# RWKV stage: ScalarE copies the turned groups out of alternating banks, the first inversion level goes by token half, and products outside the chain stand in the states' waits

## The reference

```
def step(state, inp):
    r_t, w_t, k_t, v_t, kk_t, b_t = inp
    sa = jnp.einsum('bhvk,bhk->bhv', state, -kk_t)
    state = (state * w_t[:, :, None, :] + sa[..., None] * b_t[:, :, None, :]
             + v_t[..., None] * k_t[:, :, None, :])
    y = jnp.einsum('bhvk,bhk->bhv', state, r_t)
    return state, y
...
y = rwkv7_scan(r_h, heads(decay), k_h, v_h, kk, a_h)
...
y = y + jnp.sum(r_h * k_h * r_k, axis=-1, keepdims=True) * v_h
...
y = y.reshape(B, S, RWKV_DIM).astype(p.dtype) * g
return y @ w_o_rwkv
```

## Time and profile before

| | |
|---|---|
| median of 3 runs | 1594.96 us (1594.63 to 1595.7) |
| profiled execution | 1595.48 us, its span 1594.2 us |
| TensorE matmul busy | 1536.3 us, 96% of the span |
| VectorE, ScalarE, GpSimd busy | 995.7, 643.6, 426.8 us |
| chain that ended last | PE 88%, DVE 4%, DMA 3%, ACT 2%, issue 2% |

### The profile page before, as it was taken

How to read it: one execution, slowest core, us unless ns; L and a number is a source line. 1 busy time by engine, 2 the same in 40 slices (tenths; PEclk the granted TensorE clock), 3 DMA queues, 4 the chain that set the end, 5 groups by cost and what they waited for, 6 DMA issues and landing times.

```text
span 1594.2 us, 25461 instructions
## 1 busy us (share of the span) xinstructions
PE 1536.3 (96%) x10035; PEld 1279.7 (80%) x10035; DVE 995.7 (62%) x1820; ACT 643.6 (40%) x994; POOL 426.8 (27%) x285
## 2 busy tenths in 40 slices
PE   8999999989999877899999999999999999999998
PEld 5777878765455577469999999999999888888887
DVE  5788787744465663439898843333333777777776
ACT  4455453532221411123444344334433554554543
POOL 0000000000000200004888888888885000000000
PEclk9999999999999987999999999999999999999999
DMA  9776664347465910334766656666664677777776
GB/s 338 254 260 215 230 230 134 132 158 258 140 206 184 396 73 12 109 138 146 187 145 147 143 139 144 146 145 140 141 146 110 200 243 236 243 236 244 235 244 228
DMA packets 166011, 297.25 MB, mean 186 GB/s; under 512 B 49475, under 2 KB 70259, under 8 KB 165893
## 3 DMA queue, kind: packets, MB, share of 16 engines
q1 hardware_dynamic: 119616, 277.08, 51.5%
q0 software_dynamic: 39296, 8.55, 7.3%
q10 hardware_dynamic: 6980, 9.99, 1.9%
HBM read 276.54 MB, written 19.03 MB: 185 GB/s over the span
## 4 chain that ended last, share of the span: by engine, by line
PE 88%; DVE 4%; DMA 3%; ACT 2%; issue 2%; SPq 0%; ACTq 0%; DVEq 0%
PE bank L515 21%; PE bank L517 20%; PE bank L519 20%; PE bank L510 9%; PE bank L1058 7%; PE bank L851 1%; PE bank L1005 1%; DMA ada_late<-in_w_ada_dram 1%; PE bank L488 1%; PE bank L567 1%; DMA slot<-in_w_in_dram 1%; PE bank L864 1%; DMA slot<-in_w_out_dram 1%; DVE gt L1165 1%; PE bank L863 0%
## 5 line engine op out<-in xcount | busy, mean ns | idle before, releaser
L2430 POOL DMA_INDIRECT c_dram<-gates,places x256 | 404.3, 1579 | 173.9 <-DVE gates L1831 96.3
L1184 DVE TENSOR_TENSOR dT_low<-bank,dT_high 128x512 fp32r<-128x512 f32 x256 | 165.1, 687 | 216.4 <-ACT dT_high L2327 215.0
L515 PE MATMUL bank<-hT_high,dT_high 128*128 128x256 f32 x1024 | 299.0, 292 | 0.1
L517 PE MATMUL bank<-hT_low,dT_high 128*128 128x256 f32 x1024 | 288.2, 281 | 0.0
L519 PE MATMUL bank<-hT_high,dT_low 128*128 128x256 f32 x1024 | 284.7, 278 | 0.0
L515 PE MATMUL bank<-up_high,A_high 128*128 128x512 f32 x512 | 200.0, 391 | 1.1 <-DVE A_low L1184 1.1
L517 PE MATMUL bank<-up_low,A_high 128*128 128x512 f32 x512 | 200.7, 392 | 0.0
L2339 ACT CAST up_high<-slot 128x1024 fp32r<-128x1024 f32 x128 | 134.3, 1049 | 164.2 <-DMA slot<-in_expert_up_dram 164.2
L519 PE MATMUL bank<-up_high,A_low 128*128 128x512 f32 x512 | 199.2, 389 | 0.0
L519 PEld LDWEIGHTS bank<-hT_high,dT_low 128*128 128x128 f32 x1024 | 193.4, 189 | 0.0
L515 PEld LDWEIGHTS bank<-hT_high,dT_high 128*128 128x128 f32 x1024 | 192.8, 188 | 0.3 <-issue 0.3
(11 more groups left out here) (431 smaller groups left out, 2294.6 us busy)
## 6 DMA issues: line engine op xcount, KB each, us to landing
slot<-in_expert_down_dram SPq DMA_DIRECT2D x128, 512.0 KB
slot<-in_expert_up_dram SPq DMA_DIRECT2D x128, 512.0 KB, 3.6
slot<-in_w_in_dram SPq DMA_DIRECT2D x41, 1024.0 KB, 5.2
P<-in_w_ada_dram SPq DMA_DIRECT2D x16, 1024.0 KB, 7.7
c_dram<-zeros SPq DMA_DIRECT2D x1, 16384.0 KB, 50.9
slot<-c_dram SPq DMA_DIRECT2D x128, 128.0 KB, 3.5
slot<-in_w_in_dram SPq DMA_DIRECT2D x6, 2048.0 KB, 8.2
ada_late<-in_w_ada_dram POOLq DMA_DIRECT2D x8, 1024.0 KB, 5.8
```

The source lines that it names most:

```text
L515: pe.matmul(o, lhsT=lhs_high.bitcast(F32R), rhs=rhs_high.bitcast(F32R), start=start, stop=False, skip_group_check=True)
L517: pe.matmul(o, lhsT=lhs_high.bitcast(F32R), rhs=rhs.bitcast(F32R), start=False, stop=False, skip_group_check=True)
L1184: return v.tensor_tensor(dst.bitcast(F32R), src, high, ALU.subtract)
L2430: g.indirect_dma_start(C_dram, bass.IndirectOffsetOnAxis(ap=places[:, x, k:k + 1], axis=0), gates[:, x, k:k + 1], None, compute_op=ALU.add ...
```

## The change

Four edits, and the bank numbers that they need:

1. The groups of `alphaT` and `kappaT` stay in banks 4 and 5, those of `rhoT` and `betaT` go to 6 and 7. ScalarE copies both groups of the first three; `betaT` is shared as before. The product `y = r * kx` on VectorE moves up, ahead of `alpha`.
2. Level 0 of the inversion is issued as n(0), x and y(0), n(1), kb(0), x and y(1), kb(1), instead of kb(0), n(0), n(1), kb(1), x and y(0), x and y(1). VectorE masks `D1` of a half at the end of that half, and `v_kb(0)` stands between its additions for half 0 and for half 1. Banks of x and y become 2t and 2t + 1. Levels 1 to 4 keep their order.
3. In each chunk all eight products of kappa with v are issued before the wait for U, and those of beta with U behind it.
4. `yd` of half 0 (`pe_inner(0)`) is issued behind s of chunk 1, `ys` of half 0 (`pe_outer(0)`) behind s of chunk 2; those of half 1 stay at the end. VectorE's additions stay where they were.

```
-    def pe_turn_bank(tag, tiles, k, size=4):
-        b = fill((tag, k), 4 + k % 4)
+    def pe_turn_bank(tag, tiles, k, size=4, first=0):
+        b = fill((tag, k), 4 + (first + k) % 4)
...
-            pe_turn(tag, tiles_of(x))
+            for k in range(2):
+                pe_turn_bank(tag, tiles_of(x), k, first=2 * (n % 2))
...
-        pe_pairs("kb", kappaT, 0, (6, 7))
...
+    def pe_level_xy(i, t):
+        bx, by = fill(("x", i, t), 2 * t) if i < 4 else None, fill(("y", i, t), 2 * t + 1)
...
+        pe_level_n(0, 0)
+        pe_level_xy(0, 0)
+        pe_level_n(0, 1)
+        pe_pairs("kb", kappaT, 0, (6, 7))
+        pe_level_xy(0, 1)
+        pe_pairs("kb", kappaT, 1, (6, 7))
+        for i in range(1, 5):
+            for t in range(TT):
+                pe_level_n(i, t)
+            for t in range(TT):
+                pe_level_xy(i, t)
...
+            for h in range(RH):
+                pe.matmul(o[h], lhsT=kappa[rows, t, at[h]], rhs=v_[rows, t, at[h]], start=(h < 2), stop=False,
+                          skip_group_check=True)
             for q in range(2):
                 clear(pe, ("ws", c, q))
             for h in range(RH):
...
+                m = pe.matmul(o[h], lhsT=beta[rows, t, at[h]], rhs=U[rows, t, at[h]], start=False, stop=(h > 5),
+                              skip_group_check=True)
             m.then_inc(filled(("s", c)), 1)
+            if c == 1:
+                pe_inner(0)
+            if c == 2:
+                pe_outer(0)
         for q in range(2):
             clear(pe, ("ws", 3, q))
+        pe_inner(1)
+        pe_outer(1)
...
+        v.wait_ge(shifted, 8)
+        v.tensor_tensor(y, r_, kx, ALU.mult).then_inc(bonus_raw, 1)
...
-        for tag, dst in (("alphaT", arT[:, :, 0, :]), ("rhoT", arT[:, :, 1, :]), ("kappaT", kappaT), ("betaT", betaT)):
-            v_turn(tag, by_tile(dst, 4), 2)
-            if tag == "rhoT":
-                v.tensor_tensor(y, r_, kx, ALU.mult).then_inc(bonus_raw, 1)
+        v_turn("betaT", by_tile(betaT, 4), 2)
...
-            if i == 0:
-                v_kb(0)
...
+                if (i, t) == (0, 0):
+                    v_kb(0)
...
+    def a_turn_one(tag, dst, k, size=4):
+        b = held(a, (tag, k))
+        a.copy(dst(k * size, size), b[:, 0:size * P].rearrange("p (k n) -> p k n", k=size)).then_inc(emptied((tag, k)), 1)
...
-            a_turn(tag, by_tile(dst, 4), 2)
+        for tag, dst in (("alphaT", arT[:, :, 0, :]), ("rhoT", arT[:, :, 1, :]), ("kappaT", kappaT)):
+            for k in range(2):
+                a_turn_one(tag, by_tile(dst, 4), k)
+        a_turn("betaT", by_tile(betaT, 4), 2)
```

More of the change, by code:

```diff
@@ L839, in pe_pairs @@
             m.then_inc(filled((tag, t, q)), 1)
-    def pe_invert():
-        for i in range(5):
-            for t in range(TT):
[L844 to L853, removed]
-            if i == 0:
-                pe_pairs("kb", kappaT, 1, (6, 7))
-            for t in range(TT):
[L857 to L867, removed]
@@ new lines, in pe_level_n @@
+    def pe_level_n(i, t):
+        b = fill(("n", i, t), 4 + t)
+        pe.wait_ge(level_masked, 2 * i + t + 1)
+        if i:
+            clear(pe, ("x", i - 1, t))
+            clear(pe, ("y", i - 1, t))
+        for h in range(RH):
+            for rows in HALF:
+                m = pe.matmul(b[rows, h * RN:(h + 1) * RN], lhsT=NMv[rows, t, h, :],
+                              rhs=XI[rows, t, h, :], start=True, stop=True)
+        m.then_inc(filled(("n", i, t)), 1)
+    def pe_level_xy(i, t):
+        bx, by = fill(("x", i, t), 2 * t) if i < 4 else None, fill(("y", i, t), 2 * t + 1)
+        clear(pe, ("n", i, t))
+        for h in range(RH):
+            for rows in HALF:
+                at = slice(h * RN, (h + 1) * RN)
+                if i < 4:
+                    mx = pe.matmul(bx[rows, at], lhsT=YI[rows, t, h, :], rhs=T1_[rows, t, h, :], start=True, stop=True)
+                my = pe.matmul(by[rows, at], lhsT=T1_[rows, t, h, :], rhs=YI[rows, t, h, :], start=True, stop=True)
+        if i < 4:
+            mx.then_inc(filled(("x", i, t)), 1)
+        my.then_inc(filled(("y", i, t)), 1)
@@ L908, in pe_states @@
             b = side(("s", c))
+            o = [b[HALF[h % 2], h // 2 * RN:(h // 2 + 1) * RN] for h in range(RH)]
+            at = [slice(h * RN, (h + 1) * RN) for h in range(RH)]
+            for h in range(RH):
+                pe.matmul(o[h], lhsT=kappa[rows, t, at[h]], rhs=v_[rows, t, at[h]], start=(h < 2), stop=False,
+                          skip_group_check=True)
             for q in range(2):
@@ new lines, in pe_states, with pe_inner, pe_outer @@
+        pe_outer(1)
+    def pe_inner(t):
+        b = side(("yd", t))
+        for h in range(RH):
+            for rows in HALF:
+                at = slice(h * RN, (h + 1) * RN)
+                pe.matmul(b[rows, at], lhsT=D1[rows, t, h, :], rhs=U[rows, t, at], start=True, stop=False)
+                m = pe.matmul(b[rows, at], lhsT=D2[rows, t, h, :], rhs=v_[rows, t, at], start=False, stop=True)
+        m.then_inc(filled(("yd", t)), 1)
+    def pe_outer(t):
+        for q in range(2):
+            b = side(("ys", t, q))
+            for h in odds[q]:
+                for cp in range(2):
+                    m = pe.matmul(b[HALF[cp], h // 2 * RN:(h // 2 + 1) * RN],
+                                  lhsT=arT[HALF[q], h // 2, 1, chunk(t, cp)],
+                                  rhs=states[HALF[q], 2 * t + cp, h // 2, :], start=True, stop=True)
+            m.then_inc(filled(("ys", t, q)), 1)
```

## The result

| | kernel before | changed kernel |
|---|---|---|
| first comparison, 5 runs each | 1595.7 us median (1594.63 to 1598.35) | 1585.51 us median (1579.53 to 1588.82) |
| ratio, 95% interval | | 0.9936 (0.9916 to 0.9956) |
| later, same kernel again, 5 runs | 1594.44 us (17 runs, 1591.06 to 1599.88) | 1584.41 us (1583.21 to 1587.0), ratio 0.9943 (0.993 to 0.9956) |

The change makes the kernel about 10 us faster. That is the direction and the order of size forecast (16.4 us, 1578.5), but the median lies outside the range given (1574.5 to 1584), and both kernels spread more than the three runs of before had shown.

The account below looks back on a forecast made before the run. TensorE, busy in 96% of the span, was taken as the bound, losing time in chain waits and at low clock. Savings 4.9 + 4.0 + 1.5 + 6.0 = 16.4 us gave a 1578.5 us median, range 1574.5 to 1584.

Parts of the forecast that it names:

- Turned groups: Turning ahead of the first pairs: only beta is still waited for, pairs start at 549.4 instead of 554.33, saving 4.9 us.
- First level: From the first pairs to n of level 1: 15.95 us instead of 19.99, saving 4.0 us.
- 9.5 + 0.1 + 0.95 + 1.55 + 1.87 + 1.99 = 15.95: Level 0: us to half 1's mask, start, n, kb(0), x and y of half 1, then the wait to next n.
- Levels 1 to 4: Later inversion levels: kb(1) fills the gap ahead of level 1, so its n starts at high clock, saving 1.5 us.
- Walk: Chunk loop from the states to o_mla: filled holes and a mostly high clock save 6.0 us.
- the forecast's 6.9: Chunk loop if the clock stays high: 3.2 us from moved products plus 3.7 from the clock.
- So a gain ahead of them is passed on whole: After the chunk loop: o_mla and y both start from the states' end, so all 16.4 us saved earlier remain.
- a transfer or a wait with a fixed date: After the states: something fixed in time could take back the whole gain, giving 1594 to 1596; none seen, chance 0.03.
- The bounds: Whole kernel: parts' limits 4.5 to 4.9, 0.5 to 4.0, 0 to 4.5, 1 to 6.9; range 1574.5 to 1584.
- rule on transposes: Turning ahead of the pairs: transposes do not bring full clock, so that part would give 4.5 us; judged contradicted by the trace.

Follow-up runs that it names:

- zero_early: Changed kernel with the 16 MB filling of the coefficient table with zeros issued one weight chunk earlier: 1582.85 us, ratio 0.9923.
- zero_late: Changed kernel with the zeros issued later, by ScalarE behind its copy of betaT, to run under the levels: 1591.79 us, ratio 0.9981.
- turn: Kernel before with only the alternating banks for turned groups, ScalarE's copies and the earlier product with kx: 1590.9 us, ratio 0.9982.
- walk: Kernel before with only kappa products ahead of the wait for U, and yd and ys of half 0 inside the chunk loop: 1587.79 us, ratio 0.9961.
- before_warm_m2: Kernel before with four extra unused matmuls in TensorE's wait for merged2: 1593.43 us, ratio 0.9993.
- warm_m2: Changed kernel with four extra unused matmuls in TensorE's 2.2 us wait for merged2: 1581.31 us, ratio 0.9907.
- old_level: Changed kernel with level 0 in its old order and the zeros issued one weight chunk earlier: 1585.95 us, ratio 0.9947.

## Why the prediction was wrong

- **Turned groups: right.** 5.2 to 5.8 us against 4.9 (3.6 to 5.0 against the other profiles of the old order); beta alone is waited for, the groups ran high (1.04 each), the product with kx and the sigmoids stayed hidden.
- **First level: the step that failed first.** The sum "9.5 + 0.1 + 0.95 + 1.55 + 1.87 + 1.99 = 15.95" had TensorE's pieces follow one another without a gap. I had no term for the zeros' traffic, since TensorE needed none of it. After the change the stage stops for 1.88 us between kb(0) and x and y of half 1, and `zero_early` and `zero_late` show that it is the zeros. In the profiles with the old order TensorE never stops there. In the kernel before the clock was low from 561.00 to 567.00, while the zeros ended at about 565, but in `turn` it was high from 555.87 on, with the zeros running to 560.5, and there was no stop either; there TensorE had waited 2.90 us ahead of kb(0). What spares the old order stays open. Of the other 1.1 us in the changed kernel 0.9 lie ahead of n of half 1: it started 10.5 us after the pairs instead of 9.6, with a low stretch of the clock (553.50 to 556.50) at the start of it. With the stop away the piece took 16.55, 16.66 and 16.72.
- **Levels 1 to 4: the number fits, the reason is not shown.** 1.5 us was forecast and 1.49 measured, twice, and n of level 1 starts high behind kb(1). But without kb(1) in the wait it ran high too, in `turn`, `walk` and `before_warm_m2` (2.08 us for its 64 matmuls, behind idle times of 1.99, 1.91 and 1.91 us); in the first profile of the kernel before it took 3.59 behind the same 1.91. Levels 1 to 4 took 29.93 to 32.92 us in the old order and, but for `zero_late`, 29.93 to 31.43 in the new one without extra matmuls. So most of the 1.49 us may be luck in the profile that the forecast was reckoned from.
- **Walk: right but for 0.4 us.** 6.0 forecast, 5.59 measured, with one low stretch (forecast: between none and one). The fall stands behind the hole of chunk 0; with the hole filled the walk takes 15.61, near the 15.85 that the forecast's 6.9 meant.
- **Behind the walk: the step that failed most.** "So a gain ahead of them is passed on whole" was argued from y's slack, which held (y is ready at 638.78, TensorE free for it at 639.78), and I looked for a transfer or a wait with a fixed date. I did not ask what the clock does behind a wait that stays as it is. The wait for merged2 is 2.18 us in both kernels, but only in the changed one the clock falls behind it, in all five profiles that have edits 1 to 4 with this wait unfilled (961.3 to 962.0); `warm_m2` takes the 3 us back and `before_warm_m2` does nothing. `old_level`, without edit 2, has a shorter one there (960.34); `before`, `turn` and `walk` have none. Why the fall comes there so regularly, and not in the kernel before, is not settled. In all six profiles that have it, it begins 44.4 us after the last low stretch of the walk began, so it seems to hang on where the clock fell ahead of it. That was not tested.
- **The bounds.** 16.4 less 2.4 to 3 in the first level less 3 behind is 10 to 11, which is what was measured. That the sum comes out so well is in part luck, since the column "before" varies by several us: the stage from the first turned group to o_mla took 92.45 us in it and 88.70 in `before_warm_m2`. The range missed by 0.4 to 1.5 us, because its ends had neither a stop by other transfers nor a fall of the clock behind the stage in them. The three runs shown spanned 1.1 us; 23 of the same kernel spanned 10.4.

The Trainium skill (TensorE: Matmul & The Clock Gate, A second HAM failure mode: psum-queue depth-cycling) tells of a kernel in which TensorE "micro-idles between MM groups frequently enough" that its clock goes back and forth. The traces here agree in this: the low stretches of the levels stand behind idle times of 1.99 us, and half filling them removed all of these, though what TensorE waits for here is VectorE's masks. The Trainium skill's rule on transposes (Part 4 of that page), weighed in the prediction, stays at odds with the rise to 1.00 behind nothing but turned groups. The changed kernel adds little: its groups ran in 1.04 per eight, since the clock was high already, and it fell at 553.3, just behind them.

## What to carry to other kernels

A wait that a change leaves alone can still get dearer: where TensorE's clock moves between its levels, read the granted clock behind every idle time of 1 to 2 us, also downstream of the change, and price each as one that may cost 1.5 to 3 us. A few useless matmuls in such waits (here half the wait) are a cheap remedy, and fill all of them: with some filled, part of the gain went to falls in the walk. Large transfers with no deadline should not run beside stages of many short matmuls; here they stopped TensorE, it seems by delaying its instructions. And take a part's length "before" from more than one profile where the clock moves: the same levels took 29.93 and 32.92 us.

## What I had not expected of the hardware

- With DMA queues full of a 16 MB write, TensorE stopped for 1.88, 2.03 and 3.25 us amid matmuls of 64 columns at the high clock, with nothing to wait for; levels 1 to 4 grew from 31.43 to 38.20 us. TensorE went on 1.37 to 1.58 us after a 16 KB packet of instructions had landed, in seven stops of seven.
- The clock fell behind idle times of 1.91 to 2.18 us, but not behind each: n of level 3 ran high behind 1.99 before.
- Filling 0.9 us of such waits of 2.0 us, and the hole behind chunk 0, kept the clock at 1.00 for over 1000 us.
